# Joining stage of a hybrid attention trunk: each tile loaded on its own last reader, squares ahead of weight parts, the gate row by ScalarE's queue, the first output rows fetched inside

## The reference

```python
def head_rms(o, g):
    return o * lax.rsqrt(jnp.mean(o * o, axis=-1, keepdims=True) + EPS) * g.astype(jnp.float32)

ya = merge_heads(head_rms(oa, gdn_g)) * jax.nn.silu(ga)      # oa = forward + flipped backward
yb = merge_heads(head_rms(ob, hgrn_g))                       # then column order, times sigmoid(gb)
y  = jnp.concatenate([ya, yb], axis=-1) @ w_out

x_lat = x_lat + m_lat[2] * y_lat
h_lat = modulate(rms_norm(x_lat, norm2_g[l]), m_lat[3], m_lat[4])
x_lat = x_lat + m_lat[5] * sq_relu_mlp(h_lat, w_mlp1[l], w_mlp2[l])
```

## Time and profile before

| | us |
|---|---|
| median of 3 runs | 3885.58 |
| lowest and highest | 3885.14, 3890.12 |
| profiled execution, its own time | 3882.01 |
| its span in the profile | 3880.2 |
| joining stage in it | 2291.3 to 2400.7 |
| first matmul of the output stage | 2408.31 |

### The profile page before, as it was taken

One profiled execution on the slowest core, in us unless ns is written; L12 is line 12 of the kernel. 1 busy time (PEld: TensorE's weight loads), 2 busy tenths in 40 slices (PEclk: granted clock), 3 DMA queues, 4 the chain that ended last, 5 costly groups with the idle time before them and its releaser, 6 DMA issues. The chain is left out here.

```text
span 3880.2 us, 98954 instructions
## 1 busy us (share of the span) xinstructions
PE 3376.9 (87%) x41449; PEld 2794.3 (72%) x41449; DVE 1982.7 (51%) x2884; ACT 1644.7 (42%) x2375; POOL 1675.8 (43%) x1364
## 2 busy tenths in 40 slices
PE   6899999999878888867777653999999999999998
PEld 3677888888767777756767523877887887877877
DVE  5588401110045555554455556575556556567575
ACT  5566314432145555532333412564455444323243
POOL 0220223222045545524555324545655665565564
PEclk8999999999989999996677766999999999999999
DMA  5133434453233333325343345566565557646453
GB/s 194 47 76 73 99 90 137 123 138 99 83 101 105 111 103 106 107 89 111 83 101 88 133 157 190 194 235 194 194 232 195 179 199 264 224 174 238 174 217 120
DMA packets 438927, 560.19 MB, mean 144 GB/s; under 512 B 119852, under 2 KB 355728, under 8 KB 413720
## 3 DMA queue, kind: packets, MB, share of 16 engines
q1 hardware_dynamic: 412704, 518.84, 42.1%
q10 hardware_dynamic: 20344, 21.04, 1.7%
q0 software_dynamic: 5632, 16.78, 1.5%
HBM read 354.42 MB, written 202.16 MB: 143 GB/s over the span
## 5 line engine op out<-in xcount | busy, mean ns | idle before, releaser
L2814 PE MATMUL o_pg<-o_t_hi,o_s_hi 128*128 128x512 f32 x2016 | 794.5, 394 | 60.7 <-DVE o_part L2992 18.5
L2816 PE MATMUL o_pg<-o_t_lo,o_s_hi 128*128 128x512 f32 x2016 | 790.7, 392 | 0.0
L2817 PE MATMUL o_pg<-o_t_hi,o_s_lo 128*128 128x512 f32 x2016 | 790.3, 392 | 0.0
L601 PE MATMUL p_pg<-h_hi,p_whi 128*128 128x512 f32 (+1 forms) x1384 | 530.8, 384 | 9.6 <-DVE p_wlo L830 9.6
L601 PE MATMUL p_pg<-h_hi,p_wlo 128*128 128x512 f32 (+1 forms) x1384 | 518.7, 375 | 0.0
L601 PE MATMUL p_pg<-h_lo,p_whi 128*128 128x512 f32 (+1 forms) x1384 | 518.6, 375 | 0.0
L2814 PEld LDWEIGHTS o_pg<-o_t_hi,o_s_hi 128*128 128x128 f32 x2016 | 382.2, 190 | 150.2 <-issue 38.1
L2817 PEld LDWEIGHTS o_pg<-o_t_hi,o_s_lo 128*128 128x128 f32 x2016 | 382.2, 190 | 79.9
L2816 PEld LDWEIGHTS o_pg<-o_t_lo,o_s_hi 128*128 128x128 f32 x2016 | 382.6, 190 | 79.2
L3011 DVE TENSOR_TENSOR o_s_lo<-o_raw,o_s_hi 128x512 fp32r<-128x512 f32 x288 | 263.1, 914 | 204.3 <-ACT o_s_hi L2850 204.1
L601 PEld LDWEIGHTS p_pg<-h_hi,p_whi 128*128 128x128 f32 x1384 | 261.8, 189 | 60.9 <-DVE p_wlo L830 9.8
(11 more groups left out here) (333 smaller groups left out, 6641.0 us busy)
## 6 DMA issues: line engine op xcount, KB each, us to landing
o_raw<-in_w_mlp SPq DMA_DIRECT2D x32, 1024.0 KB, 5.9
scr_f<-o_xf SPq DMA_DIRECT2D x64, 512.0 KB, 7.7
o_raw<-scr_f SPq DMA_DIRECT2D x32, 1024.0 KB, 5.4
scr_w<-o_pre SPq DMA_DIRECT2D x16, 1792.0 KB, 6.7
o_t_raw<-scr_w SPq DMA_DIRECT2D x28, 1024.0 KB, 5.5
g_kqvb<-scr_kqv SPq DMA_DIRECT2D x72, 384.0 KB, 3.5
o_xf<-scr_x SPq DMA_DIRECT2D x22, 1024.0 KB, 8.4
p_raw<-in_w_in SPq DMA_DIRECT2D x38, 512.0 KB, 5.9
```

Source lines behind the costliest of these rows:

```text
L601: last = nc.tensor.matmul(pg[0:m, bank, 0:n], w[:, q, k, 0:m], h[bank][:, k, :], start=(k == 0 and j == 0), stop=(k == KT - 1 and j == 2))
L2814: nc.tensor.matmul(out, s_hi[:, q, k, :], t_hi[:, q, k, :], start=(not more and k == 0), stop=False, skip_group_check=more)
L2816: nc.tensor.matmul(out, s_hi[:, q, k, :], t_lo[:, q, k, :], start=False, stop=False, skip_group_check=more)
L2817: last = nc.tensor.matmul(out, s_lo[:, q, k, :], t_hi[:, q, k, :], start=False, stop=(k == 3), skip_group_check=more)
```

## The change

It reorders the joining stage and moves two transfers between the stages; the arithmetic stays.

- SP: `of` and `ob` of block 1 are issued first, then weight parts 0 and 1, then `ga` of block 1. For a later block b, `ob` goes when block b - 2 is added, `of` when it is turned, `ga` and weight part b when it is gated. Semaphores `o_in` and `g_in` take the place of `load` for b >= 1; block 0 still comes under `load[0]`.
- The store of the gate rows and the spread row go by ScalarE's queue; the spread is issued after the root of block 0.
- ScalarE's order: square and root of a block stand ahead of stores and high parts.
- VectorE's order: the add of block 1 stands ahead of the scale of block 0, low parts come one block later, and only `gate(b)` waits for `ga`.
- SP fetches the first two units' rows into `o_raw` inside the joining stage, after the gate multiplies of weight parts 2 and 3 have read the tile.
- The second gate row is loaded in the output stage, after the first two `x_load`; GpSimd waits for it (`g2_in`) in `pre_piece`.

```diff
-                w_load(0)
-                w_load(1)
-                sp.wait_ge(rows_ready, 1)
-                sp.dma_start(e.sgate[:, :], mrow[:, :]).then_inc(rows_out, 16)
-                for b in range(1, NB):
...
+                o_load(1, of, 0)
+                o_load(1, ob, 1)
                 w_load(0)
                 w_load(1)
+                g_load(1)
+                for b in range(2, NB):
+                    sp.wait_ge(added, b - 1)
+                    o_load(b, ob, 1)
+                    sp.wait_ge(turned, b - 1)
+                    o_load(b, of, 0)
+                    sp.wait_ge(gated, b - 1)
+                    g_load(b)
+                    w_load(b)
                 for q in range(2):
                     sp.wait_ge(e.s_stored[q], 32)
-                sp.wait_ge(wo_joined, 16)
-                sp.dma_start(e.o_gate[:, :].rearrange("p (k d) -> p k d", k=KT),
-                             e.sgate[3 * KT:4 * KT, :].unsqueeze(0).to_broadcast([P, KT, P])).then_inc(gate_in, 16)
+                sp.wait_ge(stored[0], 16)
+                for i in range(2):
+                    sp.wait_ge(wo_gated, 3 + i)
+                    e.o_raw_load(sp, i)
...
+                act.dma_start(e.sgate[:, :], mrow[:, :]).then_inc(rows_out, 16)
+                square(0)
+                roots(0)
+                act.wait_ge(rows_out, 16)
+                act.dma_start(e.o_gate[:, :].rearrange("p (k d) -> p k d", k=KT),
+                              e.sgate[0:KT, :].unsqueeze(0).to_broadcast([P, KT, P])).then_inc(gate_in, 16)
+                square(1)
+                roots(1)
+                store(0)
+                square(2)
+                roots(2)
+                w_high(0)
+                store(1)
+                square(3)
+                roots(3)
+                w_high(1)
+                store(2)
+                w_high(2)
+                store(3)
+                w_high(3)
...
+                    if b >= 1:
+                        dve.wait_ge(g_in[p], 16 * ((b + 1) // 2))
...
+                add(0)
+                sums(0)
+                add(1)
+                scale(0)
+                sums(1)
+                gate(0)
+                scale(1)
+                add(2)
+                sums(2)
+                gate(1)
+                scale(2)
+                w_low(0)
+                add(3)
+                sums(3)
+                gate(2)
+                scale(3)
+                w_low(1)
+                gate(3)
+                w_low(2)
+                w_low(3)
...
-                raw_load(0)
                 x_load(0)
-                raw_load(1)
                 x_load(1)
+                sp.dma_start(gate[:, :].rearrange("p (k d) -> p k d", k=KT),
+                             e.sgate[3 * KT:4 * KT, :].unsqueeze(0).to_broadcast([P, KT, P])).then_inc(g2_in, 16)
...
+        def raw_load(sp, i):
+
+            sp.dma_start(e.o_raw[:, i % 2].rearrange("p a c -> p (a c)").rearrange("p (k t) -> p k t", k=KT),
+                         e.sy[:, :, 2 * P * i:2 * P * (i + 1)].rearrange("k p t -> p k t")).then_inc(e.o_raw_in[i % 2], 16)
```

More of the change, by code:

```diff
@@ L2367, in phase_merge @@
         wo_in = [sem("y_wo0"), sem("y_wo1")]
+        o_in, g_in = [sem("y_o0"), sem("y_o1")], [sem("y_g0"), sem("y_g1")]
         wo_gated, wo_joined, wo_hi, wo_lo = (sem("y_" + n) for n in ("wo_g", "wo_j", "wo_hi", "wo_lo"))
@@ L2377, in w_load, with o_load, g_load @@
                                      quadrants(e.w_out[0], kk)[:, n]).then_inc(wo_in[kk % 2], 16)
+                def o_load(b, t, d):
+                    sp.dma_start(t[b % 2][:, :, :, :], e.so[d, CCH + b * G:CCH + (b + 1) * G].rearrange("n p a d -> p n a d")
+                                 ).then_inc(o_in[b % 2], 16)
+                def g_load(b):
+                    sp.dma_start(ga[b % 2][:, :, :], e.sga[:, :, b * TB:(b + 1) * TB].rearrange("a p t -> p a t")).then_inc(g_in[b % 2], 16)
@@ L2379, in _ @@
+                o_load(1, of, 0)
+                o_load(1, ob, 1)
                 w_load(0)
                 w_load(1)
-                sp.wait_ge(rows_ready, 1)
-                sp.dma_start(e.sgate[:, :], mrow[:, :]).then_inc(rows_out, 16)
-                for b in range(1, NB):
[L2384 to L2392, removed]
-                        sp.dma_start(e.o_gate[:, :].rearrange("p (k d) -> p k d", k=KT),
-                                     e.sgate[0:KT, :].unsqueeze(0).to_broadcast([P, KT, P])).then_inc(gate_in, 16)
-                    if b >= 2:
-                        w_load(b)
+                g_load(1)
@@ L2422, in store, with square @@
                     act.dma_start(e.sy[0:PAIRS, :, b * TB:(b + 1) * TB].rearrange("a p t -> p a t"), y[:, b % 2]).then_inc(stored[b % 2], 16)
-                act.wait_ge(rows_turned, 1)
-                nc.scalar.activation(mrow[:, :], pt[0:32, 1, 0, 0:P], ACT.Copy).then_inc(rows_ready, 1)
-                for b in range(NB):
+                def square(b):
                     act.wait_ge(added, b + 1)
@@ L2430, in _, with roots, w_high @@
                     nc.scalar.activation(sq[:, :, :, :], of[b % 2][:, :, :, :], ACT.Square).then_inc(squared, 1)
+                def roots(b):
                     act.wait_ge(summed, b + 1)
                     nc.scalar.activation(ms[:, :, :], ms[:, :, :], ACT.Sqrt, bias=e.eps[:, :], scale=1.0 / HD).then_inc(root, 1)
[L2433 to L2440, removed]
+                def w_high(kk):
+                    act.wait_ge(wo_joined, 4 * kk + 4)
+                    nc.scalar.activation(t_hi[:, :, kk, :], lo32[:, :, kk, :], ACT.Copy).then_inc(wo_hi, 1)
+                act.wait_ge(rows_turned, 1)
+                nc.scalar.activation(mrow[:, :], pt[0:32, 1, 0, 0:P], ACT.Copy).then_inc(rows_ready, 1)
+                act.wait_ge(rows_ready, 1)
+                act.dma_start(e.sgate[:, :], mrow[:, :]).then_inc(rows_out, 16)
[18 more added lines that the diff above has]
+                w_high(3)
             @block.tensor
@@ L2472, in w_low, with add, sums @@
                     dve.tensor_tensor(t_lo[:, :, kk, :], lo32[:, :, kk, :], t_hi[:, :, kk, :].bitcast(F32), ALU.subtract).then_inc(wo_lo, 1)
-                for b in range(NB):
+                def add(b):
                     p = b % 2
-                    dve.wait_ge(load[p], 48 * (b // 2 + 1))
+                    if b == 0:
+                        dve.wait_ge(load[0], 48)
+                    else:
+                        dve.wait_ge(o_in[p], 32 * ((b + 1) // 2))
                     dve.tensor_tensor(of[p][:, :, :, :], of[p][:, :, :, :], ob[p][:, :, :, :], ALU.add).then_inc(added, 1)
+                def sums(b):
                     dve.wait_ge(squared, b + 1)
@@ L2481, in _, with scale @@
                     dve.tensor_reduce(ms[:, :, :], sq[:, :, :, :], AX_X, ALU.add).then_inc(summed, 1)
-                    if b >= 1:
-                        gate(b - 1)
+                def scale(b):
+                    p = b % 2
                     dve.wait_ge(root, b + 1)
@@ L2517, in phase_out @@
         BANK = (BX, BY, BX, BY, BV, BZ, BV)
-        raw_in, x_in = [sem("raw0"), sem("raw1")], [sem("x%d" % i) for i in range(3)]
+        raw_in, x_in = e.o_raw_in, [sem("x%d" % i) for i in range(3)]
+        g2_in = sem("g2")
         mixed, s_hi_ready, s_lo_ready = sem("mixed"), sem("s_hi"), sem("s_lo")
@@ L2599, in raw_load @@
                     if i < M1:
-                        src = e.sy[:, :, 2 * P * i:2 * P * (i + 1)].rearrange("k p t -> p k t")
-                    elif i < M2:
+                        e.o_raw_load(sp, i)
+                        return
+                    if i < M2:
                         j = (i - M1) % (N1 // 2)
@@ L3061, in phase_tail @@
         e.o_gate = nc.alloc_sbuf_tensor_at("o_gate", [P, D], F32, offset=e.o_gate_at)
+        e.o_raw_in = [ctx.enter_context(nc.semaphore("o_raw%d" % i)) for i in range(2)]
+        def raw_load(sp, i):
+            sp.dma_start(e.o_raw[:, i % 2].rearrange("p a c -> p (a c)").rearrange("p (k t) -> p k t", k=KT),
+                         e.sy[:, :, 2 * P * i:2 * P * (i + 1)].rearrange("k p t -> p k t")).then_inc(e.o_raw_in[i % 2], 16)
+        e.o_raw_load = raw_load
         phase_merge(nc, e)
```

7 lines of the change are left out of this document (1 added, 6 removed).

## The result

The changed kernel took 3847.52 us (median of 4 runs, 3836.34 to 3851.1) beside 3885.36 for the kernel before (4 runs, 3875.6 to 3890.12): ratio 0.9907, interval 0.9887 to 0.9927, about 38 us less, with 28 to 44 possible. The forecast was 3852.6, in a range of 3842 to 3862. The 28 to 44 reach from about the gain of the second rival (28) to that of the first (43): the whole time alone can't choose between them and the forecast, the profile has to. Its profiled execution took 3849.12 us, with a span of 3847.3.

The account below looks back on a forecast made before the run. The joining stage was taken as wholly on the path, paced by order and loads, then by the VectorE-GpSimd port. Gains of 27.4 plus 5.6 us made 33.0: 3849 against the profiled 3882.0, 3852.6 as a median, range 3842 to 3862.

Parts of the forecast that it names:

- second rival: Joining stage: gate row lands no earlier, port idle 5 us; gain 28 us, kernel 3857.7 us; chance 0.13.
- first rival: Joining stage: no VectorE-GpSimd port exclusion, only latency; gain 43 us, kernel 3842.6 us; chance 0.12.
- Step 1: Joining stage: block 1's loads, ahead of the weight parts, land about 2302 instead of 2308.3 us.
- Step 2: VectorE adds block 1 before scaling block 0: block 0 turned six microseconds later, hidden by block 1's earlier square.
- Step 3: Gate row by ScalarE's queue lands at 2307 us, within 2302 to 2309, instead of 2312.2.
- Step 4: Joining stage from 2307.0: shared port work, GpSimd 38.9 plus VectorE 27.0, sums to 65.9 us; stage ends at 2373.
- Step 5: Joining stage: later loads keep up; block 2's output by 2319.4, weight parts 2 and 3 at 2330 and 2350.4 us.
- third rival: Joining stage: weight parts 2 and 3 late by 3 us each, last high half uncovered; gain 24, kernel 3861.5; chance 0.12.
- Step 6: Output rows 0 and 1 fetched inside the joining stage: 5.64 us removed behind it, input rows x covered.

Follow-up runs that it names:

- run 1: Changed kernel with the gate row back on SP's queue, store behind weight parts 0 and 1, spread behind ga of block 1: stage 87.8 us, whole 3861.81 us.
- run 8: Changed kernel with only the earlier fetch of weight part 3, ahead of the forward output of block 3: stage 79.0 us, whole 3847.45 us.
- run 2: Changed kernel with the first two fetches of output rows back at the head of the output stage: stage 78.7 us, whole 3855.89 us.
- runs 5 and 6: Changed kernel with two extra VectorE instructions, ahead of block 2's add and scale: reductions (5) stage 78.7 us, whole 3841.27; two-SBUF-input adds (6) 84.5, 3846.88.
- Orders alone: Kernel before with only the new orders of ScalarE and VectorE, loads and SP's order as before: stage 105.4 us, whole 3884.01 us.
- loads alone: Changed kernel with the old orders of ScalarE and VectorE; loads, gate row and output rows as changed: stage 92.6 us, whole 3868.12 us.
- with the reductions: Changed kernel with two extra VectorE reductions, ahead of the add and the scale of block 2: stage 78.7 us, whole 3841.27 us.
- with part 3 early: Changed kernel with only weight part 3 fetched earlier, ahead of the forward output of block 3: stage 79.0 us, whole 3847.45 us.

## Why the prediction was right, step by step

The mechanism was right: the joining stage lies wholly on the path, its waits were waits for order and loads, and behind them the port between VectorE and GpSimd is what is left. It forecast 33.0 us, and start of stage to end of span gave 37.0: 3.0 more in the stage (30.4 for 27.4) and 1.0 more behind it (6.6 for 5.6). The terms:

- Step 1, the loads of block 1: forecast 10.7 us into the stage, measured 10.5. Taking off 3 us for each of the 2 MB no longer in front, by the landings of the earlier trace rows, gave the right time.
- Step 2, six microseconds lost on block 0: the transposes began 15.5 us into the stage (9.8 before) and nothing waited for them but gate 0. Hidden, as said: the port was full with GpSimd's first part meanwhile.
- Step 3, the gate row: taken at 15.7 us, measured 7.0 + 6.6 = 13.6. It was not the last to come: weight part 0 was there at 14.6, and the port, held by the scale, free at 15.4. Moving the row to ScalarE's queue is worth 9.0 us (run 1); the rival priced its failure at 5, since it counted only the idle time at the start (6.0 in run 1) and not the high and low parts left uncovered at the end (3.2). The Trainium skill (DMA: Bandwidth & Descriptors, Issuing engines are not separate DMA queues) allows a second issuer nothing but issue time. No run here shows a higher rate from one, and most of what it gave was issue time: in run 1 the 16 KB store was issued 7.0 us into the stage, once SP had issued the loads in front of it, and took 8.9 us, where ScalarE issued it at 0.8 us and it took 6.2; the spread had to wait for it. What the second queue gave is an order. Run 1 changed the queue and the place together, so it doesn't show whether a store early on SP's own queue would do as well.
- Step 4, the port: forecast 65.9 us from the moment it is full, measured 63.4. Of the sum 38.9 stood for GpSimd with gaps between its instructions; in the trace the gaps come to almost nothing, and at each change of hands the next instruction ends about 0.13 us early (1.13 for a join of 1.26), some fifteen times, 2 us. This term was mis-sized by 2.5 us. With a start 0.3 us earlier (15.4 us into the stage, not 15.7) and the 0.2 by which the walk came out above its own sum, the stage is 3.0 shorter than the 81.8 forecast.
- Step 5, the loads keep up: the forward output of block 2 landed in 6.0 us (5.64 taken), at 2322.57, as VectorE came free (2322.56), and 4.4 us before the port did; weight parts 2 and 3 came 3 to 4 us before GpSimd asked. The third rival never began, and run 8 shows that a still earlier part 3 gives nothing.
- Step 6, the fetch inside: 5.6 forecast, 5.1 between run 2 and the changed kernel, 6.6 between the two profiles of before and after; to the first product it is 5.7 (7.85 to 2.17 us). x did not take its place. The time behind the stage differs by up to 4 us among runs with the same output stage, so the difference between 5.1 and 6.6 is not explained here.
- The first rival (no exclusion, 3842.6) is about as near to the measured 3847.52 as the forecast (4.9 us against 5.1) and is wrong in mechanism: runs 5 and 6. That the measured median lies between the two says nothing for either.
- What the forecast did not say: how little the parts are worth alone. Orders alone bring 3.8 us, loads alone 16.6.

## What to carry to other kernels

When waits for loads and waits behind another engine's order alternate, undoing one kind shows the other; judge such edits together, or by the stage in the profile. Before moving work between VectorE and GpSimd, add up all that needs their common port (GpSimd's instructions and VectorE's with two SBUF inputs). In this stage that sum, less 0.13 us for each change of hands, was the floor; reductions (2286 ns) and multiplies out of PSUM (2347 ns) kept their length beside it, and an engine handed a faster piece of work can lose it again by where it stands in a written-out order. A small row that everybody waits for goes where no megabytes are in front of it; here that was another engine's queue.

## What had not been expected

The stretch ahead of the stage, the same code in all kernels, ended anywhere from 2287.6 to 2304.9 us in the fourteen profiles of this study, while start of the stage to end of the span was 1551.7 and 1551.9 in the two profiles of the changed kernel, 1551.9 with the reductions and 1552.5 with part 3 early. Most of the scatter between these profiles therefore comes from before the stage. The traces narrow it down: the last product of the projection starts between 1054.7 and 1057.6 us in all fourteen, the first of the HGRN2 chunks (L1794) between 1787.2 and 1804.1, and the last of them between 2173.6 and 2190.8. From the one to the next it takes 731 to 747 us, and through the HGRN2 chunks 380 to 392: the scatter arises in these two stretches of scans, and its cause stays open. For an edit worth a few microseconds, the profile from the edit's place on tells more than the whole times, which spread over 18 us for the changed kernel.
